# Order of the high-part and low-part products inside the up projections of the feed-forward stages

## The reference, cut to what matters

```python
up = causal_dwconv(h2 @ w_up[i], conv_w[i], conv_b[i])       # first block
g_ff, v_ff = up[..., :D_FF], up[..., D_FF:]
x = x + (jax.nn.silu(g_ff) * v_ff) @ w_down[i]

def swiglu_half(h, w1, w3, w2):                               # second kind, two per block, two blocks
    return 0.5 * ((jax.nn.silu(h @ w1) * (h @ w3)) @ w2)
```

## Time and profile before

| | |
|---|---|
| median of 3 runs | 1581.9 us |
| profiled execution, first to last instruction (span) | 1579.9 us |
| PE busy | 1563.3 us, 99% |
| PEld busy | 1362.7 us, 86% |
| DVE busy | 1098.9 us, 70% |
| ACT busy | 862.8 us, 55% |
| granted TensorE clock | 1.000 on average |
| line 879 (B) | 1600 matmuls |
| line 886 (L) | 1600 matmuls |

### The profile page before, as it was taken

The page is one execution under the profiler, slowest core; times in us unless marked ns, Lnnn a source line. Parts: engine busy times, 40 slices in busy tenths (PEclk is TensorE's granted clock), DMA queues, the critical chain, the costliest instruction groups (busy, mean ns, idle before and its releaser), DMA issues.

```text
span 1579.9 us, 22509 instructions
## 1 busy us (share of the span) xinstructions
PE 1563.3 (99%) x9026; PEld 1362.7 (86%) x9026; DVE 1098.9 (70%) x1396; ACT 862.8 (55%) x1002; POOL 97.5 (6%) x92
## 2 busy tenths in 40 slices
PE   9999999999999999999999999999999999999998
PEld 7988898888888888898889888888888988888887
DVE  7889767787877666654667666676666547676665
ACT  8877574665575444555446444554445544464443
POOL 1135200000000000010100000000000101000000
PEclk9999999999999999999999999999999999999999
DMA  7889956455457555453544555355554535545552
GB/s 305 258 225 281 283 170 242 146 204 189 184 166 259 189 187 187 167 180 133 204 182 162 202 188 206 139 213 205 177 194 162 185 144 186 187 173 213 182 191 80
DMA packets 43679, 305.36 MB, mean 193 GB/s; under 512 B 4928, under 2 KB 5312, under 8 KB 7360
## 3 DMA queue, kind: packets, MB, share of 16 engines
q1 hardware_dynamic: 39696, 279.61, 49.0%
q0 software_dynamic: 2880, 20.97, 6.5%
q10 hardware_dynamic: 1008, 3.41, 0.6%
HBM read 302.93 MB, written 1.05 MB: 192 GB/s over the span
## 4 chain that ended last, share of the span: by engine, by line
PE 88%; DVE 5%; DMA 3%; ACT 2%; issue 1%; SPq 0%; POOL 0%; POOLq 0%; ACTq 0%; DVEq 0%
PE pairs L879 22%; PE pairs L886 11%; PE pairs L658 8%; PE pairs L660 8%; PE pairs L659 8%; PE big L658 7%; PE big L660 7%; PE big L659 7%; PE pairs L900 2%; DMA wlo<-weights 2%; DVE wlo L579 1%; DVE ar L1881 1%; PE pairs L908 1%; DVE ar L1889 1%; PE big L709 1%
## 5 line engine op out<-in xcount | busy, mean ns | idle before, releaser
L579 DVE TENSOR_TENSOR wlo<-raw,whi 128x2048 fp32r<-128x2048 f32 x239 | 548.0, 2303 | 186.3 <-ACT whi L565 184.1
L565 ACT ACTIVATE whi<-raw 128x2048 fp32r<-128x2048 f32 x259 | 492.7, 1910 | 127.1 <-PE big L660 74.1
L879 PE MATMUL pairs<-h_both,whi 128*128 128x512 f32 x1600 | 407.7, 392 | 0.4 <-DVE wlo L579 0.3
L879 PEld LDWEIGHTS pairs<-h_both,whi 128*128 128x128 f32 x1600 | 290.4, 189 | 53.1 <-DVE wlo L579 1.3
L1419 ACT ACTIVATE ar<-pairs 128x512 f32<-128x512 f32 x137 | 81.3, 595 | 276.7 <-PE pairs L879 224.0
L886 PEld LDWEIGHTS pairs<-h_both,wlo 128*128 128x128 f32 x1600 | 218.3, 190 | 15.6
L886 PE MATMUL pairs<-h_both,wlo 128*128 128x256 f32 x1600 | 223.1, 282 | 0.0
L658 PE MATMUL big<-whi,b_hi 128*128 128x512 f32 x452 | 177.5, 393 | 0.5 <-DVE wlo L579 0.4
L660 PE MATMUL big<-whi,b_lo 128*128 128x512 f32 x452 | 176.2, 390 | 0.0
L659 PE MATMUL big<-wlo,b_hi 128*128 128x512 f32 x452 | 175.9, 389 | 0.0
L1881 DVE TENSOR_TENSOR ar<-pairs,ar 128x512 f32<-128x512 f32 (+1 forms) x124 | 90.7, 732 | 98.3 <-ACT ar L1419 89.1
(11 more groups left out here) (257 smaller groups left out, 2085.9 us busy)
## 6 DMA issues: line engine op xcount, KB each, us to landing
raw<-weights SPq DMA_DIRECT2D x262, 1024.0 KB, 4.8
wlo<-weights POOLq DMA_DIRECT2D x20, 1024.0 KB, 14.8
ar<-consts ACTq DMA_DIRECT2D x1, 2112.0 KB, 11.3
ar<-mem SPq DMA_DIRECT2D x2, 512.0 KB, 5.4
raw<-weights SPq DMA_DIRECT2D x4, 256.0 KB, 5.9
x_rows<-x SPq DMA_DIRECT2D x1, 1024.0 KB, 10.5
ar<-ssm_bc SPq DMA_DIRECT2D x1, 512.0 KB, 13.5
ar<-g_final ACTq DMA_DIRECT2D x1, 512.0 KB, 3.6
```

The costliest lines, as they stand in the source:

```text
L565: act.activation(whi[:, slot(u), :], raw[:, u % RING, :], ACT.Copy).then_inc(S("hi_done"), 1)
L579: dve.tensor_tensor(wlo[:, slot(u), :], raw[:, u % RING, :], whi[:, slot(u), :].bitcast(F32), ALU.subtract)\
L879: return pe.matmul(out, w(k, l, (half * KD + kk) * P, P)[0], h_both[:, kk, :, :].rearrange("p a t -> p (a t)"), start=kk == 0, stop=kk == ...
```

## The change

Inside each half of an up unit, the 256-column products are no longer in one group; each L follows the B of its input block. The order becomes B0 L0 B1 L1 ... B6 L6 L7 B7. The number of products, their operands, their start and stop marks and all semaphores are the same.

```diff
+                        def low(kk):
+                            pe.matmul(out[:, 0:TOK], w(k, l, (half * KD + kk) * P, P)[1], h_hi[:, kk, :],
+                                      start=False, stop=False)
+
                         for kk in range(KD - 1):
                             both(kk)
-                        for kk in range(KD):
-                            pe.matmul(out[:, 0:TOK], w(k, l, (half * KD + kk) * P, P)[1], h_hi[:, kk, :],
-                                      start=False, stop=False)
+                            low(kk)
+                        low(KD - 1)
                         last = both(KD - 1)
                     fin(last)
```

## The result

The changed kernel takes 1587.02 us (median of 7 runs, 1586.63 to 1587.82), against 1581.91 us before (7 runs beside it). The ratio is 1.003, with a 95% interval of 1.002 to 1.0039: slower by 5.1 us. The forecast was 1580.2, a gain of 1.7 us.

What follows compares the result with a forecast made beforehand. PE's product-to-product distances in the up units were taken as the bound: -1.8 us over 160 halves and +0.1 over 40 gave -1.7, span 1578.2, plus 2.0 for the median, 1580.2; range 1570 to 1590.

Steps and rivals of the forecast that it cites:

- What bounds the kernel: Inside the up units nothing is waited for; PE is 99% busy, and time is the distance from product to product.
- The settled distances and the sums of a half now: Up units before the change: B 0.2275 us, L 0.120 (0.1133 with short load); a half 2.793, behind a down unit 2.773.
- L between two B's, 0.114: Alternating up-unit halves: an L takes 0.114 us, as L0 does, from bounds of 0.114 and 0.120.
- B between two L's, 0.233: Alternating up-unit halves: a B takes 0.233 us, as B7 first behind L's, from bounds of 0.227 and 0.233.
- The missing 0.007 stands at the B that follows: In alternation a 0.120 load does not fit under an L of 0.113, so B pays; a pair stays 0.347 us.
- What is left to gain is the slow stretch: Slow B's after an L run, beyond their first 0.006 us, would go: 0.011 us less per half, 160 times, -1.8 us.
- slow rival: Up units: each pair pays both borders, L 0.120 and B 0.233; 7.0 us more, 1588.9; chance 20%.
- fast rival: Up units: every load gets a B's slack, L 0.114 and B 0.227; 11.0 us less, 1570.9; chance 25%.
- third rival: Up units: order indifferent, the slow stretch spreads evenly over the pairs, a half stays 2.793 us; 1581.9; chance 12%.

Runs made afterwards that it cites:

- run per unit: The order of before, but the two halves of an up unit share one run of L's: 1580.33 us, ratio 0.999 to before.
- version by pairs: The order of before, but the two up units of a pair share one run of L's: 1582.04 us, ratio 0.9998 to before.

## Why the prediction was wrong

- **What bounds the kernel:** right. The B's of the up units waited 0.4 us in all before and after, the L's not at all, and the whole effect is in the distances.
- **The settled distances and the sums of a half now:** right. The 0.227, 0.120 and 0.1133 come back in the experiments (0.2267 in the run per unit), and the versions with fewer changes came out within 0.4 us of sums made with them, but for the version by pairs with its wait and its lower clock. One reading was off: B0, the second B behind L's, was read as 0.233 like B7, and by the starts of the same trace it is 0.236.
- **L between two B's, 0.114:** wrong, and the larger part of the miss. The pairs of the changed kernel have 0.12 in each of the timeline's rows, the mean over all L's is 281 - 163 = 118 ns, and by the starts L0 to L6 have 0.117: 0.003 x 7 x 200, about 4 us.
- **B between two L's, 0.233:** wrong. 398 - 163 = 235 ns on average, and 848.85 to 849.09 is 0.24: 0.002 x 7 x 200, about 3 us. I took the two bounds for bounds, but they were the first step of a course each (the step after it, B0's 0.236, already lay above my upper one), and each product of an alternating stream starts where the one before has left it. This is the step that failed: the mean pair is 0.352 in place of 0.347, 0.005 x 7 x 200 = 7.0 us, where the forecast and the result lie 1.7 + 5.1 = 6.8 us apart.
- **"The missing 0.007 stands at the B that follows", by which a pair costs the same:** wrong as a mechanism. A full load goes beside an L of 0.113 when L's own load is short, and now and then when it is not. A pair loses 0.015 when L is 384 columns long and has 0.05 us of room for the load.
- **What is left to gain is the slow stretch:** right in itself, since fewer changes gained just that, but the alternation has more changes, not fewer. The same rows that showed the stretch said so: it begins anew at each change from L to B. That was in the slow rival's "for", and I gave it 20%.
- **The slow rival:** nearly right in the sum (0.353 per pair against 0.352, 7.0 us against 5.1), wrong in its reason: L was not held at 0.120 by a load and B was not at 0.233. It put L too high and B too low, and the two errors cancelled; that was luck.
- **The fast rival:** loads stayed one ahead, and with full loads the pair of 0.341 came only in about a tenth of the cases. The third rival, no change at all, is excluded by the interval of the ratio. "TensorE: Matmul & The Clock Gate" of the Trainium skill gives the distance of products by their columns ("Back-to-back issue gap") and the load by its columns ("LDWEIGHTS"), so by it the order is indifferent; the table above disagrees, 7.5 us between its ends.

Still open is what in the engine runs this course. Shown are these: it depends on the lengths of the products and of the loads beside them (or of the rows that a load of 64 columns leaves out), it ends in equal streams after about five products, it may end in an alternation if loads are short (pairs of 0.34) and does not with full loads (B's mean stays at 398 ns), what ran before a half changes it, and the place of operands and result is without effect. That a load and a moving read share some resource is a guess that would fit, but no run shows the resource.

## What to carry to other kernels

In a TensorE-bound stream with full 128-column loads, keep products of equal length together and the runs long: each change from 256 to 512 columns between long runs cost about 0.02 us here, and alternation cost 0.005 us per pair above the settled sum with 256 columns and 0.015 above the columns with 384. Do not price a new order by the first product behind a border in the old one; where the trace has only borders, take the sum over the whole settling course as the cost and expect it at every border between long runs; between short ones it is less. Longer runs move waits forward, so look at the stage where the weights come late before merging two units: here one wait of 1.8 us, with the lower clock behind it, took back the gain of 49 pairs.

## What the runs showed of the hardware that was not expected

- A 512-column and a 256-column product in turn, with full loads: 0.352 us per pair on average (0.340 to 0.361) against 0.347 settled. With loads of 64 columns on either side 0.343 and 0.344 on average, with long stretches at 0.340, the sum of the columns alone (0.2267 + 0.1133).
- 0.120 us of an L run is not the least that a 128-column load needs beside a product: with short and full loads in turn, 0.113 did.
- A change in the length of the loads alone slows a stream of equal products: seven B's behind a down unit take 1.61 us in place of 1.59.
- Behind one wait of 1.8 us of TensorE the granted clock was 0.50, and 32 L's took 5.31 us in place of 3.83.
- A product of 384 columns between products of 512 lost more (0.109 us per half above the columns) than one of 288 (0.066), though it leaves every load more room.
